# Matrix memory's scores as two rounded matmuls from stacked keys and remainders, and the heads' roots moved behind their weighings on ScalarE

## The reference, cut to what matters

```
def mlstm_chunkwise(q, k, v, log_i, log_f, state0):
    ...
        b = jnp.cumsum(fc, axis=-1)
        logw = jnp.where(lower, b[..., :, None] - b[..., None, :] + ic[..., None, :], -jnp.inf)
        ...
        s = jnp.einsum('bhtd,bhsd->bhts', qc, kc) * jnp.exp(logw - m_t[..., None])
        num = w_inter[..., None] * jnp.einsum('bhvd,bhtd->bhtv', C, qc) + jnp.einsum('bhts,bhsv->bhtv', s, vc)
        den = w_inter * jnp.einsum('bhd,bhtd->bht', n, qc) + jnp.sum(s, axis=-1)
        h = num / jnp.maximum(jnp.abs(den), jnp.exp(-m_t))[..., None]

def odd_mixer(...):
    ...
    def readout(hf, hb, o):
        h = jnp.swapaxes(hf + rev(hb), 1, 2)
        B, T = h.shape[:2]
        h = rmsnorm(h, out_g).reshape(B, T, -1).astype(o.dtype)
        return jnp.dot(h * jax.nn.sigmoid(o), w_out)
```

## Time and profile before

| what | value |
|---|---|
| median of 3 executions | 2792.58 us (2789.26 to 2794.09) |
| the profiled execution | 2792.33 us, its span 2790.6 us |
| TensorE matmul, share of the span | 95% |
| VectorE, ScalarE, GpSimd | 54%, 33%, 10% |
| granted TensorE clock, mean | 0.985 |
| DMA, mean | 85 GB/s |

### The profile page before, as it was taken

One profiled execution on the slowest core, in us unless ns is written; L12 is line 12 of the kernel. 1 busy time (PEld: TensorE's weight loads), 2 busy tenths in 40 slices (PEclk: granted clock), 3 DMA queues, 4 the chain that ended last, 5 costly groups with the idle time before them and its releaser, 6 DMA issues. The chain is left out here.

```text
span 2790.6 us, 32311 instructions
## 1 busy us (share of the span) xinstructions
PE 2663.0 (95%) x13354; PEld 2164.4 (78%) x13354; DVE 1515.6 (54%) x2047; ACT 914.6 (33%) x1222; POOL 284.6 (10%) x160
## 2 busy tenths in 40 slices
PE   7998999899999999999988999999999899999998
PEld 5876666688888888888767888888676678888887
DVE  6227899874338536472266543444689833533332
ACT  4332434423211212252266332332333622332221
POOL 2111223000000000000000000000240644000000
PEclk9999999999999999999999999999999999999999
DMA  7011001431215414122001222323120222222321
GB/s 275 21 52 53 31 32 45 151 136 61 74 63 185 161 60 191 46 81 101 18 1 39 83 85 104 106 70 112 61 84 16 76 100 87 86 97 93 106 82 62
DMA packets 37037, 236.10 MB, mean 85 GB/s; under 512 B 4128, under 2 KB 5152, under 8 KB 13216
## 3 DMA queue, kind: packets, MB, share of 16 engines
q1 hardware_dynamic: 36896, 234.11, 23.4%
HBM read 231.99 MB, written 2.10 MB: 84 GB/s over the span
## 5 line engine op out<-in xcount | busy, mean ns | idle before, releaser
L369 PE MATMUL pair<-h_high,w_high 128*128 128x512 f32 x1984 | 715.9, 369 | 15.7 <-ACT w_high L301 8.6
L370 PE MATMUL pair<-h_low,w_high 128*128 128x512 f32 x1984 | 710.8, 367 | 0.0
L323 DVE TENSOR_TENSOR w_low<-ring,w_high 128x2048 fp32r<-128x2048 f32 (+5 forms) x164 | 342.3, 2092 | 193.7 <-ACT w_high L301 186.4
L375 PE MATMUL pair<-h_high,w_low 128*128 128x512 f32 x1984 | 444.3, 366 | 0.7 <-POOL w_low L323 0.7
L369 PEld LDWEIGHTS pair<-h_high,w_high 128*128 128x128 f32 x1984 | 374.7, 189 | 82.8 <-issue 12.8
L370 PEld LDWEIGHTS pair<-h_low,w_high 128*128 128x128 f32 x1984 | 375.0, 189 | 64.5 <-issue 1.7
L375 PEld LDWEIGHTS pair<-h_high,w_low 128*128 128x128 f32 x1984 | 345.9, 189 | 63.0 <-POOL w_low L323 1.1
L301 ACT ACTIVATE w_high<-ring 128x2048 fp32r<-128x2048 f32 (+4 forms) x167 | 289.9, 1737 | 309.8 <-PE pair L375 203.9
L369 PE MATMUL pair<-high,w_high 128*128 128x512 f32 (+1 forms) x704 | 249.1, 363 | 1.0 <-DVE low L1280 1.0
L370 PE MATMUL pair<-low,w_high 128*128 128x512 f32 (+1 forms) x704 | 249.0, 363 | 0.0
L1274 DVE TENSOR_TENSOR gate<-gate,pair 128x512 f32<-128x512 f32 (+1 forms) x66 | 51.3, 777 | 238.4 <-PE pair L375 223.2
(11 more groups left out here) (464 smaller groups left out, 4017.1 us busy)
## 6 DMA issues: line engine op xcount, KB each, us to landing
ring<-in_w_up SPq DMA_DIRECT2D x66, 1024.0 KB, 4.8
ring<-in_w_ada SPq DMA_DIRECT2D x32, 1024.0 KB, 4.8
ring<-in_w_down SPq DMA_DIRECT2D x32, 704.0 KB, 4.0
ring<-in_w_ada0r SPq DMA_DIRECT2D x16, 1024.0 KB, 4.7
ring<-in_w_merge_b SPq DMA_DIRECT2D x14, 1024.0 KB, 4.8
ring<-in_w_down SPq DMA_DIRECT2D x8, 1024.0 KB, 4.8
ring<-in_w_att_in SPq DMA_DIRECT2D x6, 1024.0 KB, 4.8
ring<-in_w_heads SPq DMA_DIRECT2D x6, 1024.0 KB, 4.9
```

What stands on the lines that cost most here:

```text
L323: (on or self.nc.vector).tensor_tensor(self.w_low[:, n % 2, 0:floats], self.ring[:, chunk % RING, 0:floats], self.w_high[:, n % 2, 0:float ...
L369: self.nc.tensor.matmul(out[:, a:e], w_high[:, k, at], high[:, k, a:e], start=k == 0, stop=False)
L370: self.nc.tensor.matmul(out[:, a:e], w_high[:, k, at], low[:, k, a:e], start=False, stop=False)
L375: mm = self.nc.tensor.matmul(out[:, a:e], w_low[:, k, at], high[:, k, a:e], start=False, stop=k == kt - 1)
```

## The change

The scores are no longer float32 matmuls. Keys and queries are each written as a rounded part and a remainder, both in the rounded float32 type. For a head, `kS` holds in the head's own 64 rows the rounded keys and in the other 64 rows the keys' remainders; `qS` holds the rounded queries in both. One matmul over 128 rows gives rounded keys by queries plus remainders of keys by queries, and a second over 64 rows adds the rounded keys by the queries' remainders (`qL`). The product of the two remainders is left out.

Heads 1 to 7 are staged by GpSimd, with five instructions each in place of one. Head 0 is staged by ScalarE (two roundings) and VectorE (one copy and two subtractions) before their other work. The zeroing of `qS` goes, and the first spread waits only for the two copies into `both`. On ScalarE, `root` of the head stands behind all weighings of the next but one, where before it stood behind the weighing of job 2.

```
--- before.py
+++ after.py
@@ -195,6 +195,8 @@
         self.norm_high = sem("norm_high")
         self.norm_low = sem("norm_low")
         self.tail_lat = sem("tail_lat")
+        self.head_high = sem("head_high")
+        self.head_low = sem("head_low")
         self.last_divided = sem("last_divided")
         self.last_read = sem("last_read")
         self.last_added = sem("last_added")
@@ -3067,7 +3069,12 @@
     hs = lambda t: K.xT[:, t // 2, LAT + P * (t % 2):LAT + P * (t % 2) + P]
     with ExitStack() as stack:
         sb = lambda name, shape: stack.enter_context(K.temp(name, shape))
-        qS = sb("qS", [P, 2, LAT])
+
+
+        half = lambda name, shape: stack.enter_context(K.temp(name, shape, F32R))
+        kS, qS, qL = half("kS", [P, 2, ALL]), half("qS", [P, 2, LAT]), half("qL", [P, LAT])
+        own = lambda h: slice(64 * (h % 2), 64 * (h % 2) + 64)
+        other = lambda h: own(h + 1)
         prob = sb("prob", [P, 2, 2, 6 * LAT])
         hn, junk = sb("hn", [P, 4, P]), sb("junk", [P, P])
         den, ss = sb("den", [P, 2, 4]), sb("ss", [P, 4])
@@ -3086,19 +3093,20 @@
         @block.gpsimd
         def _(pool):
             chain = Chain(pool, K.pool_chain)
-            for half in range(2):
-                r = slice(64 * half, 64 * half + 64)
-                chain.step(nc.gpsimd.tensor_copy(both[r, :], K.ident[r, r]))
-            chain.sync()
-            for b in range(2):
-                chain.step(nc.gpsimd.memset(qS[64 - 64 * b:128 - 64 * b, b, :], 0.0))
-            chain.sync()
-            for h in range(HEADS):
-                b, r = h % 2, slice(64 * (h % 2), 64 * (h % 2) + 64)
+            nc.gpsimd.tensor_copy(both[0:64, :], K.ident[0:64, 0:64])
+            nc.gpsimd.tensor_copy(both[64:P, :], K.ident[64:P, 64:P]).then_inc(staged.sem, 1)
+            for h in range(1, HEADS):
+                b, r, o = h % 2, own(h), other(h)
                 if h >= 2:
 
                     pool.wait_ge(scored.sem, scored.base + JOBS * (h - 1))
-                nc.gpsimd.tensor_copy(qS[r, b, :], qT[r, h // 2, :]).then_inc(staged.sem, 1)
+                chain.step(nc.gpsimd.tensor_copy(qS[r, b, :], qT[r, h // 2, :]))
+                chain.step(nc.gpsimd.tensor_copy(kS[r, b, :], kT[r, h // 2, :]))
+                nc.gpsimd.tensor_copy(qS[o, b, :], qT[r, h // 2, :])
+                chain.sync()
+                nc.gpsimd.tensor_tensor(qL[r, :], qT[r, h // 2, :], qS[r, b, :].bitcast(F32), ALU.subtract)
+                nc.gpsimd.tensor_tensor(kS[o, b, :], kT[r, h // 2, :], kS[r, b, :].bitcast(F32),
+                                        ALU.subtract).then_inc(staged.sem, 1)
             chain.close()
 
         @block.tensor
@@ -3117,13 +3125,17 @@
 
             def score(h, j):
                 g, s = JOBS * h + j, order[j]
-                if j == 0:
+                if j == 0 and h == 0:
+                    pe.wait_ge(K.head_low.sem, K.head_low.base + 1)
+                elif j == 0:
                     pe.wait_ge(staged.sem, staged.base + h + 1)
                 if g >= 2:
 
                     pe.wait_ge(mixed.sem, mixed.base + g - 1)
-                nc.tensor.matmul(scores(g), kT[:, h // 2, s * P:s * P + P], qS[:, h % 2, :],
-                                 start=True, stop=True).then_inc(scored.sem, 1)
+                b, keys = h % 2, slice(s * P, s * P + P)
+                nc.tensor.matmul(scores(g), kS[:, b, keys], qS[:, b, :], start=True, stop=False)
+                nc.tensor.matmul(scores(g), kS[own(h), b, keys], qL[own(h), :],
+                                 start=False, stop=True).then_inc(scored.sem, 1)
 
             def weighted_sums(h, n):
                 if n == 0:
@@ -3209,6 +3221,8 @@
                 nc.scalar.activation(ss[:], ss[:], ACT.Exp, scale=-0.5).then_inc(rooted.sem, 1)
                 chain.close()
 
+            nc.scalar.activation(qS[own(0), 0, :], qT[own(0), 0, :], ACT.Copy).then_inc(K.head_high.sem, 1)
+            nc.scalar.activation(kS[own(0), 0, :], kT[own(0), 0, :], ACT.Copy).then_inc(K.head_high.sem, 1)
             for h in range(-1, HEADS):
                 ahead, back = h + 1 < HEADS, h >= 1
                 if ahead:
@@ -3218,12 +3232,10 @@
                     read_first(h - 1)
                 if ahead:
                     weigh_corners(h + 1)
-                    weigh(h + 1, 2)
+                    for j in range(2, JOBS):
+                        weigh(h + 1, j)
                 if back:
                     root(h - 1)
-                if ahead:
-                    for j in range(3, JOBS):
-                        weigh(h + 1, j)
 
             nc.scalar.activation(K.root[:], K.eps[:], ACT.Sqrt)
 
@@ -3292,6 +3304,13 @@
                 nc.vector.scalar_tensor_tensor(yT[:, h, 0:LAT], turns, K.v("out_g", h), sig[:, h, :],
                                                ALU.mult, ALU.mult).then_inc(out_ready.sem, 1)
 
+            r, o = own(0), other(0)
+            dve.wait_ge(K.head_high.sem, K.head_high.base + 1)
+            nc.vector.tensor_copy(qS[o, 0, :], qT[r, 0, :])
+            nc.vector.tensor_tensor(qL[r, :], qT[r, 0, :], qS[r, 0, :].bitcast(F32), ALU.subtract)
+            dve.wait_ge(K.head_high.sem, K.head_high.base + 2)
+            nc.vector.tensor_tensor(kS[o, 0, :], kT[r, 0, :], kS[r, 0, :].bitcast(F32),
+                                    ALU.subtract).then_inc(K.head_low.sem, 1)
             dve.wait_ge(K.loaded.sem, K.loaded.base + 16)
             open_corners(0)
             for h in range(HEADS + 1):
@@ -3319,7 +3338,7 @@
     for c, n in ((spread, HEADS), (scored, JOBS * HEADS), (summed, 3 * HEADS), (turned, HEADS - 1),
                  (weighed, JOBS * HEADS), (rooted, HEADS - 1), (first_read, 4 * HEADS - 4), (mixed, JOBS * HEADS),
                  (den_ready, HEADS - 1), (added, 4 * HEADS - 4), (normed, HEADS - 1), (diag_ready, HEADS),
-                 (out_ready, HEADS - 1), (staged, HEADS)):
+                 (out_ready, HEADS - 1), (staged, HEADS), (K.head_high, 2), (K.head_low, 1)):
         c.base += n
 
 
```

## The result

The changed kernel took 2810.99 us (median of 4 executions, 2807.79 to 2813.61), the kernel before 2790.92 (4 executions, 2788.46 to 2794.09). The ratio is 1.0073, with a 95% interval of 1.0061 to 1.0085: 20 us slower, where the forecast was 7.2 and the range ended at 2808. The direction was right, and the size was off by a factor of nearly three.

A forecast was written before the change was run, and what follows sets the result against it. Turns were taken as bound by a chain through TensorE, VectorE and ScalarE, the root just in time for the transposes. Terms 7.4 - 0.8 - 0.4 + 0.0 + 1.0 = +7.2 us gave 2799.5, range 2794 to 2808.

The forecast's parts named there:

- The scores: TensorE's score matmuls: 0.86 us each becomes 0.47, saving 0.39; only scores 2 and 3 of a head's six on the path.
- T: Start of a head's weighted sums on TensorE; one turn runs from one such start to the next, 16.67 us before.
- the -0.8 of head 1: Head 1's turn, which has no transposes and so was to keep its gain from shorter scores: -0.8 us.
- The roots: ScalarE's root, 1.68 us later, delays VectorE's norm and TensorE's transposes: +1.24 us a head, +7.4 in heads 2 to 7.
- The clock: TensorE's clock falls near most turns' sums: 0 in heads 2 to 7, swallowed by the transposes' stand; +1.0 us in head 1.
- there already: The clock fall at the last head's sums, present in the kernel before, so given no new cost.
- The start: Stage start: corners +0.5 us from staging head 0, about -0.5 from spread 1 and a shorter score; 0.0 in all.
- TensorE's passes decide: Rival: root not late for the transposes, seven turns gain 0.78 us each, 2786.7 us, faster; chance 0.12.
- Paid back in part: Rival: squares and weighings overlap better, root 1.0 us late, 0.56 a head, 2795.7 us, no measurable change; chance 0.20.
- The clock falls twice a turn: Rival: the 2.0 us stand before the transposes also lowers the clock, +8.4 us over six heads, 2808 us; chance 0.13.
- The port: Rival: GpSimd's subtractions stretch VectorE's work before the next sums by up to 2.4 us, seven times, 2816 us; chance 0.05.

The follow-up runs named there:

- experiment 3: Changed kernel with the second score pass over all 128 rows, the other half of the queries' remainders zero: 2800.32 us, ratio 1.0033.
- experiment 4: Changed kernel with each score as a thrown-away 64-row pass, the 64-row pass, then the 128-row pass: 2809.55 us, one execution.
- experiment 1: Kernel before, float32 scores kept, with only ScalarE's root moved behind all weighings: 2801.03 us, ratio 1.0044.
- experiment 8: Kernel before with the root behind all weighings and the transposes behind the third group of sums, output step moved likewise: 2788.31 us, ratio 0.9994.
- experiment 2: Changed kernel with the root put back behind the weighing of job 2: 2808.78 us, ratio 1.0068.
- experiment 9: Changed kernel with 128-row second pass, later transposes and output step: first run 2792.96 us; second, adding thrown-away passes and small matmuls at the start, 2784.53 us.
- experiment 7: Changed kernel with thrown-away passes ahead of scores 0, 1, 4, 5 and small thrown-away matmuls around head 0's first two scores: 2803.04 us, ratio 1.0047.
- experiment 6: Changed kernel with thrown-away passes ahead of scores 0, 1, 4 and 5: 2809.28 us, ratio 1.0064.

## Why the prediction was wrong

**The two scores on the path.** One of the two steps that failed is in "The scores": "so two such passes cost 0.47", with the second taken at a full pass's 0.23 "as columns are what both passes stream". I named the old 0.86 as the upper bound and said that no row shows the form; the bound was nearly the truth. The pair takes 0.84 us in the trace, so of a forecast saving of 0.39 a score 0.02 came. In each turn with transposes the corners start at T + 12.83 and not at T + 12.38. Of these 0.45 us 0.37 are the pair, 2.2 us in six turns, and the -0.8 of head 1 is gone. Experiments 3 and 4 show the cause: two changes between 64 and 128 rows for each score, 0.29 us. The other 0.08 us is that two passes of one form take 0.55 and not 0.47.

**The roots.** Right, in mechanism and size. The move was forecast at 1.68 us, and experiment 1 measured a turn of +1.72 with the old scores and +11.4 us in all; experiment 8 took it away by moving the waiting instruction. In the changed kernel the norm at T + 7.99 and the transposes at T + 8.74 are within 0.03 us of the forecast. But to name it as the cause of the loss was only half right: experiment 2 loses 19.1 us without it. It is sufficient and not necessary, and in the changed kernel it costs little of its own, 1.0 us by the medians.

**The clock.** The other step that failed, and the larger one, is in "The clock": the falls in heads 2 to 7 were put at 0 ("so up to 1.4 us is swallowed: 0"), the one in head 1 at +1.0, the last one at nothing new, and the start of the stage had no term for the clock at all. "I expect a fall in most turns near T" came true, and a fall of 3.4 us was indeed swallowed by the stand in front of the transposes, in the three turns of 18.36 to 18.37 us. But that the falls came at all was in part luck. They were expected because halved scores would stretch TensorE's idle pieces to 2.3 and 1.0 us; the scores kept their length, the pieces are 1.70 and 0.68 us (before, 1.50 and 0.47), and the clock fell all the same. What I had not forecast is that every second fall lasts 6.8 us: then TensorE comes to the transposes at T + 9.7, a whole 1 us behind the norm, and the turn grows by 0.95. The long falls started 1.0 to 1.2 us ahead of T, the short ones 0.1 to 0.3 us behind it.

Over heads 2 to 7 the account in the forecast's own terms closes: 6 x 1.24 for the roots, 6 x 0.45 for the later corners (0.37 the pair, the rest left over by the rows), 3 x 0.95 for the long falls and -0.25 behind head 7's transposes (7.62 us to the last T, 7.87 before) make 12.7, measured 10.30 + 2.36 = 12.66. It is one way to book them: in experiment 2 falls and pairs bring TensorE to the transposes nearly as late without any late root. The last T's fall was "there already", but of 3.4 us and not 6.8: +0.96. The other runs bear this out. From the last T to the end of the sums it is 8.3 and 8.7 us where no fall lies there (experiment 9's first run, experiment 7), 9.9 to 10.4 with one of 3.4 us, and 11.3 to 11.5 with one of 6.8.

**The start and head 1.** The corners came as forecast (+0.34 for +0.5). But from 1370.17 to 1390.65 TensorE stayed at 1.2 GHz, where before it was back after two falls of 3.4 us. Head 1's turn holds 5.2 us of that, worth 2.6 at half speed, and it grew by 2.57; I had given its clock +1.0. Experiments 6 and 7 show how much hangs on this stretch: with it at 1.00 the first T comes 3.6 us earlier at equal thrown passes, and head 1's turn is 16.13 us, as good as before.

**The rivals.** *TensorE's passes decide* lost: the root was late, and the passes were no shorter. *Paid back in part* lost: the overlap of squares and weighings is the computed one. *The clock falls twice a turn* came nearest in time (2808) but not in its mechanism: in the changed kernel no second fall came in the stand, and in experiment 1 a stand of 1.62 us brought none either. It is not ruled out in itself, for experiment 7 shows one such fall behind a stand of 1.62 us, with a price of 1.6 us. *The port* fell in the turn: five GpSimd instructions of 5.1 us lie beside the end of VectorE's corners, mixes 4 and 5, divisors and second direction (1437.64 to 1442.90); the corners take 2.16 us as before and the mixes 1.67 for 1.68. At the start it is real: VectorE's two subtractions took 1.21 and 1.27 us where they take 0.69 and 0.95 alone, and GpSimd's took 1.89 for 1.28 us when it met VectorE. The Trainium skill, "SBUF — State Buffer", section "Who interferes with whom", has this lock between the two; these rows agree with it.

**The sum.** The forecast had 7.4 of its 7.2 us from the roots and treated the rest as small. The stage lost 17.6 us, 10.4 more than forecast. About 3.5 of these are the passes (6 x 0.45 and head 1's 0.8) and 6.8 the clock (1.4 at the start, most of it behind the corners, 1.6 in head 1, 2.85 in the long falls, 0.96 at the last T). Costs do not add up here: roots alone +11.4, scores alone +19.1, both +20.1. The scores' part is a change of form (9.5 us between experiment 3 and the changed kernel, falls that went with it included) and the clock (6.6 us or more by experiment 7), and these two overlap with the roots and with each other. Open is why the low clock lasts 3.4 us in one turn and 6.8 in the next. The 2.4 us between the stage's and the span's difference are within what the same instructions scatter outside the stage.

## What to carry to other kernels

A matmul whose form (rows of the array) differs from its neighbours' pays at each change of form; here 0.29 us for the two changes ate nearly all that a score of two rounded passes saved (0.84 us for 0.86, where full rows take 0.55), and padding with zeros to the same rows was faster. An instruction moved later on one engine costs what waits for it: look for the waiting instruction and move that too, as the late transposes did, which turned +11.4 us into no loss. And work taken off TensorE in a stage where it waits for other engines can cost more than it saves by the clock: check the granted clock of the stage first, and price thrown work against it.

## What the runs showed of the hardware

The granted clock did not follow how long the records of TensorE were busy. The kernel before, in its turns (stretch of the same columns):

```profile
1446.00:1449.30 3.30, 1.80 (x6) 0.52 (x4) 3.12 (x12) 0.93 (x2) 0.61 (x1) 1.00 0.00 0
```

After these 3.3 us with records over 1.80 of them the clock stayed at 1.00; in the changed kernel records lay over 1.84 of the 3.3 us from 1438.50, and 0.50 came. 17.70 us of records in 20.4 us, at the start of the changed kernel, did not bring it back, and 18.16 in 20.3 were at 1.00 throughout in experiment 7. TensorE's idle piece ahead of score 0 was 1.50 us before and 1.70 in the changed kernel, and the 1.62 us stand of experiment 1 came on top of such a piece without any fall; behind one such stand of experiment 7 there was one. What of TensorE's work the chip goes by is left open. That thrown matmuls can pay for themselves is shown by the two runs of experiment 9, 8.4 us apart; in experiment 6, put where the clock was low already, they paid for nothing.
